# Release of the first expert slots in halves, and a shorter routing chain, in a two-block transformer kernel on one core

## The chip, the cores and the metric

The kernel runs on one core of a Trainium2 chip. The metric is the device time of one execution in microseconds (us). The kernel before takes 778.24 us, the median of 3 runs (778.0 to 778.46).

## The reference

Two transformer blocks of width 1024 over 256 tokens, all in float32. The first block mixes three branches (pooling, latent attention, attention over a memory), adds them to x, and then runs a mixture of experts; the second block is an attention block with a gated feed-forward part. The change lies in the mixture of experts, cut to what matters:

```
g_idx = argmax(g_logits)                       # one of 4 groups, per token
e_sel = e_logits of the 8 experts of that group
top_p, top_i = top_k(softmax(e_sel), 2)
weights = p_g * top_p / sum(top_p)
y = sum over the 2 experts e: weight * (silu(h @ w_gate[e]) * (h @ w_up[e])) @ w_down[e]
```

There are 32 experts, each with a gate matrix and an up matrix of 1024 x 256 and a down matrix of 256 x 1024: three matrices of 1 MiB each. The gains of the norms are folded into the copies that turn the tokens.

## The kernel before, in words

Each engine has its own program, written out by hand in order. They meet at named points: `up(name)` counts a semaphore up, `at(name)` is the wait for it, and `own()` is the wait of an engine for its own last counted instruction.

**Loads.** SyncE (SP) alone issues loads, in one fixed order. Weights go to slots of 1 MiB. A slot is refilled by `fetch` (L496) when the weight in it has been used (`released`). The 96 expert matrices come in the order gate, up, down for each group of four experts; 28 slots are in the ring, so that loads run ahead of the products. The four slots that hold the gate matrices of experts 0 to 3 are refilled in another way, by `fetch_parted` (L504): four quarters each, 2 KB in each of the 128 partitions, quarter by quarter over the four slots, so 16 loads of 256 KB. The quarters wait for the points `taken part 0`, `taken part 1`, `taken part 2` and `taken eg 0`. The matrices that these 16 loads bring are laid out in DRAM in quarters by `laid`. Their place in the queue is behind the load into X (a down matrix, which waits for `h2`) and ahead of the loads into the slots of the up matrices of experts 0 to 3, which wait for `taken eu 0`. The last four up matrices are loaded in halves of 4 KB in each partition by `fetch_last_up` (L514).

**Routing.** VectorE (DVE) works on rows of 4 and 32 numbers for 2 x 128 tokens: logits (L2058), group maximum (L2061), the rank of the first group that has it (L2064, L2067), a mask of the other groups (L2070) which is added to the expert logits (L2074), the two largest of them (L2080), the negated maximum for ScalarE's exponentials (L2083), marking of the two (L2084, L2087), and the 0/1 matrix M (L2090). TensorE (PE) sums M over tokens to give each token its place at its expert (L987 to L989, point `rank`) and the number of tokens of each expert (L991, L992, point `count`). DVE adds the places (L2095) and makes the one-hot matrix `hot` of group 0 (`select`, L2138, point `sel`).

**First expert group.** `begin_experts` on PE waits for `sel 0`, then gathers the tokens of experts 0 to 3 in four parts (`gather_first`, L1021, two of eight tiles of 128 columns each) and multiplies each part by its quarter of the gate matrices (`first_gates`, L1030). DVE copies parts 0 and 1 from PSUM (L2170), ScalarE (ACT) copies parts 2 and 3 (L1610). The order is gather 0, gather 1, gates 0, gather 2, gates 1, gather 3, gates 2, gates 3. Each `first_gates(n)` releases quarter n of the four slots.

**Idle products.** `warm(n, bank)` (L642) issues n matrix products of the constants, whose results nobody reads. `WARM[3]` = 10 of them stand between the logits and the rank, `WARM[4]` = 4 between the count and the first gathering.

**Later groups.** `experts(g)` (L1067) does the gate and up products of group g, `gather(g + 1)` (L1003) gathers for the next one, `experts_down` (L1090) and `combine` (L1100) finish the group. The last group is done expert by expert (L1120, L1129). Behind it the second block follows; its weights are behind the experts' in SP's queue.

Of the kernel before, what the change touches and what calls it, by code (L numbers as in the profile page):

```python
# [10 lines left out]
ALU = mybir.AluOpType  # L11
# [11 lines left out]
FILL_M = 2  # L23
FILL_B = (1, 2, 1, 2) * 3
TILE_AT = {12: 0, 13: 1, 14: 2, 15: 3, 16: 4, 17: 5, 18: 6}
WARM = (9, 6, 9, 10, 4, 6)
FFN_AT = ((0, 0), (1, 0), (2, 0), (3, 0), (6, 0), (7, 0), (0, 1), (1, 1))
CAP = 32
NEG = -1.0e30
# [14 lines left out]
def shape_constants():  # L44
    c = np.zeros((P, C_END), np.float32)
    c[:, C_ID:C_ID + P] = np.eye(P)
    c[:, C_TRI:C_TRI + P] = np.triu(np.ones((P, P)), 1)
    c[:, C_ONE] = 1.0
    causal = np.where(np.tril(np.ones((P, P))) > 0, 0.0, NEG)
    c[:, C_MASK + P:C_MASK + 2 * P] = causal  # L50
    c[:, C_IOTA:C_IOTA + CAP] = np.arange(CAP)
    c[:, C_RANK:C_RANK + 4] = 4 - np.arange(4)
    c[:, C_INVF:C_INVF + 32] = (np.float32(1.0) / (np.float32(10000.0) ** (np.arange(0, 64, 2, dtype=np.float32) / np.float32(64)))).astype(np.float32)
    pool = np.zeros((4, 256, 256), np.float32)
    for g, w in enumerate((2, 4, 8, 16)):
        for s in range(256):
            n = min(s + 1, w)
            pool[g, s + 1 - n:s + 1, s] = np.float32(1.0) / np.float32(n)
            pool[g, s, s] -= 1.0
    pool = np.ascontiguousarray(pool.reshape(4, 2, P, 256).transpose(2, 1, 0, 3)).reshape(P, 2048)  # L60
    return c, pool


class Points:
# [19 lines left out]
    def at(self, name, *key):  # L84
        return (self.sems[name], self.value[name, key]) if self.real else (None, 1)

    def own(self):

        return self.latest
# [22 lines left out]
class Weights:  # L112
# [25 lines left out]
    def plan(self):  # L138


        freed = [u for u in range(self.dense_end) if self.units[u][2]]
        self.slot, self.before, self.nth = [0] * self.dense_end, [None] * self.dense_end, []
        for n, u in enumerate(freed):
            self.slot[u] = n % DENSE
            self.before[u] = freed[n - DENSE] if n >= DENSE else None
        apart = [u for u in range(self.dense_end) if not self.units[u][2]]
        for n, u in enumerate(apart):
            self.slot[u] = DENSE + n
        left = [(self.slot[u], u) for u in freed[-DENSE:]]
        uses = [max(q for q in range(self.dense_pieces) if q % PIECES // 2 == z) for z in range(2)]  # L150
        self.half_first = uses.index(min(uses))
        self.half_use = min(uses)
        near, far = ([(RAW + z, None) for z in (h, 2 + h)] for h in (self.half_first, 1 - self.half_first))
        ring = ([(RAW - 1, None)] + [(self.slot[u], u) for u in apart] + [(RAW + EXT + z, None) for z in (1, 2, 3)]
                + [(RAW + z, None) for z in (8, 9, 4, 5)] + left[:1] + [(RAW + EXT + BIG, None), (RAW + 7, None)]
                + left[1:3] + [(RAW + EXT, None)] + left[3:] + near + far + [(RAW + 6, None), (RAW + EXT + BIG + 1, None)])
        order = [ring[n % len(ring)][0] for n in range(self.expert_end - self.dense_end)]
        held = dict(ring)
        for n, m in ((-16, -4), (-15, -3)):
            order[n], order[m] = order[m], order[n]  # L160
        for u, z in zip(range(self.dense_end, self.expert_end), order):
            self.slot.append(z)
            self.before.append(held[z])
            held[z] = u
        left = [u for u in range(self.expert_end - len(ring), self.expert_end) if self.slot[u] < RAW]
        for u in range(self.expert_end, len(self.units)):
            n = u - self.expert_end
            self.before.append(left[n] if n < RAW else u - RAW)
            self.slot.append(self.slot[self.before[u]])
        times = {}  # L170
        self.parted = [u for u in range(self.dense_end, self.expert_end)
                       if self.key.get(self.before[u]) in [("eg", n) for n in range(4)]]
        self.last_up = [self.raws["eu", n] for n in range(28, 32)]
        for u, z in enumerate(self.slot):
            times[z] = times.get(z, 0) + (64 if u in self.parted else 16)
            self.nth.append(times[z])
        self.final = {}
        for q, p in enumerate(self.pieces):
            self.final[p.unit] = q

    def laid(self):


        self.begin, parts, n = {}, [], 0
        for u, (src, _, _) in enumerate(self.units):
            if not self.dense_end <= u < self.expert_end:
                self.begin[u] = n
                parts.append(np.ascontiguousarray(src).reshape(-1))
                n += parts[-1].size
            elif u in self.parted:  # L190
                self.begin[u] = n
                parts.append(np.ascontiguousarray(src.reshape(P, 4, 512).transpose(1, 0, 2)).reshape(-1))
                n += parts[-1].size
        return np.concatenate(parts)

# [88 lines left out]
def program(nc, ctx, x, xT, mem, memT, positions, gate_b, grow, w_route, b_route, rel_ext, cst, out, wt, dense,  # L284
# [201 lines left out]
    def sync(e, real):  # L486
# [10 lines left out]

        def fetch_parted():

            for a in range(4):  # L500
                for u in wt.parted:
                    e.wait_ge(*(at("taken", "part", a) if a < 3 else released(wt.before[u])))
                    first = wt.begin[u] + 512 * P * a
                    e.dma_start(slot_view(u).rearrange("p k n -> p (k n)")[:, 512 * a:512 * a + 512],  # L504
                                dense[first:first + 512 * P].rearrange("(p m) -> p m", p=P)).then_inc(s_slot[wt.slot[u]], 16)

        def fetch_last_up():

# [120 lines left out]
    def tensor(e, real):  # L629
# [354 lines left out]
        warm(WARM[3], 3)  # L984
        enter(2, "ranked")
        e.wait_ge(*at("M"))
        e.matmul(bank[2][:, 0:32], tri, M[:, 0, :], start=True, stop=True)  # L987
        e.matmul(bank[2][:, 32:64], ones, M[:, 0, :], start=True, stop=False)
        e.matmul(bank[2][:, 32:64], tri, M[:, 1, :], start=False, stop=True).then_inc(*up("rank"))  # L989
        enter(0, "counted")  # L990
        e.matmul(bank[0][:, 64:96], ones, M[:, 0, :], start=True, stop=False)  # L991
        e.matmul(bank[0][:, 64:96], ones, M[:, 1, :], start=False, stop=True).then_inc(*up("count"))  # L992
# [32 lines left out]
        def first_gates(n):  # L1025

            e.wait_ge(*at("XE dve" if n < 2 else "XE act", "part", n))
            for kk in (2 * n, 2 * n + 1):
                for j in range(4):
                    t = e.matmul(bank[0][32 * j:32 * j + 32, 0:256], XE[:, kk, 32 * j:32 * j + 32],  # L1030
                                 slot_view(wt.raws["eg", j])[:, kk, :], start=(kk == 0), stop=(kk == 7))
            t.then_inc(*(up("taken", "part", n) if n < 3 else up("taken", "eg", 0)))

        def begin_experts():

            e.wait_ge(*at("sel", 0))
            e.wait_ge(*at("h2", 1))
            gather_first(0)
            gather_first(1)
            enter(0, "expert a", 0)  # L1040
            for n in range(4):
                e.wait_ge(*landed(wt.raws["eg", n]))
            first_gates(0)
            gather_first(2)
            first_gates(1)
            gather_first(3)
            first_gates(2)
            first_gates(3)
# [711 lines left out]
    def vector(e, real):  # L1760
# [306 lines left out]
        e.tensor_reduce(tm_, OG, AX, ALU.max).then_inc(*routed())  # L2067
        e.wait_ge(*own())
        for i in range(2):
            t = e.tensor_scalar(OG[:, i, :], OG[:, i, :], tm_[:, i, :], NEG, ALU.is_lt, ALU.mult)  # L2070
        t.then_inc(*routed())
        e.wait_ge(*own())
        for i in range(2):
            t = e.tensor_tensor(EM[:, i, :].rearrange("p (g k) -> p g k", g=4),  # L2074
                                el[:, i, :].rearrange("p (g k) -> p g k", g=4),
                                OG[:, i, :].unsqueeze(2).to_broadcast([P, 4, 8]), ALU.add)
        t.then_inc(*routed())
        e.wait_ge(*own())
        for i in range(2):
            t = e.max(top[:, i, :], EM[:, i, :])  # L2080
        t.then_inc(*routed())
        e.wait_ge(*own())
        e.tensor_scalar(nm, top[:, :, 0:1], -1.0, None, ALU.mult).then_inc(*up("expert maximum"))  # L2083
        e.memset(top[:, :, 2:8], ABSENT).then_inc(*routed())  # L2084
        e.wait_ge(*own())
        for i in range(2):
            t = e.match_replace(TT[:, i, :], top[:, i, :], EM[:, i, :], TAKEN)  # L2087
        t.then_inc(*routed())
        e.wait_ge(*own())
        e.tensor_scalar(M, TT, TAKEN, None, ALU.is_equal).then_inc(*up("M"))  # L2090
        e.wait_ge(*own())
        e.tensor_scalar(PX, M, -1000.0, 1000.0, ALU.mult, ALU.add).then_inc(*routed())
# [39 lines left out]
        def select(g):  # L2132

            if g:
                e.wait_ge(*at("gathered", g - 1, 1))
                e.wait_ge(*at("sel weights", g - 1))
            for i in range(2):
                t = e.tensor_tensor(hots[i], iota, of_four(PX[:, i, :], g), ALU.is_equal)  # L2138
            t.then_inc(*up("sel", g))

        def select_weights(g):

# [409 lines left out]
```

## Time and profile before

| | |
|---|---|
| median of 3 runs | 778.24 us (778.0 to 778.46) |
| the profiled execution | 778.07 us, of which the span is 776.3 us |
| PE busy | 731.0 us, 94% of the span |
| DVE busy | 420.0 us, 54% |
| ACT busy | 337.9 us, 44% |
| loads | 206.07 MB, mean 265 GB/s |
| granted TensorE clock, mean | 0.988 |

The span is the time from the first to the last instruction of the trace, and all places in the trace are in us from its start. The granted clock is the part of TensorE's full 2.4 GHz that was granted in a stretch (0.5 is 1.2 GHz). The DMA share is the mean busy share of the 16 DMA engines. The chain that ended last is followed back from the last instruction, at each step to what released it. Rows of TensorE overlap, and in a group the busy time is that of the group, not the sum.

### The profile page before, as it was taken

The page shows a single profiled execution, that of the slowest core. Times are in us where ns is not written, and L with a number is a line of the kernel's source. Part 1 is how long each engine was busy: PE and PEld are TensorE (multiplying, and loading weights), DVE is VectorE, ACT ScalarE, POOL GpSimd, SP SyncE. Part 2 cuts the span into 40 slices and gives each one's busy share as a digit, 9 for nine tenths or more (in the row PEclk, how much of TensorE's full clock was granted, in tenths as well). Part 3 has the DMA queues.
Part 4 walks back from the last instruction along what each step waited for, and adds up shares of the span by engine and source line. Part 5 has one row for each costly group of instructions (what it writes and reads, how often), then busy time and mean ns, then how long its engine had stood idle before and what let it go on. Part 6 is the DMA issues. An engine that isn't in the chain of part 4 may idle for free.

```text
span 776.3 us, 12463 instructions
## 1 busy us (share of the span) xinstructions
PE 731.0 (94%) x5138; PEld 601.7 (78%) x5138; DVE 420.0 (54%) x747; ACT 337.9 (44%) x604; POOL 32.4 (4%) x65
## 2 busy tenths in 40 slices
PE   8999999999999999999675879999999999999997
PEld 8898888888788866666343549999778888888885
DVE  5667756667666421111010208666668776777675
ACT  5966565554444421110010127555656434344433
POOL 2700000000000000000000001000001000000000
PEclk9999999999999999999988999999999999999999
DMA  8953557347988899999999998953434464555201
GB/s 340 415 211 118 206 218 285 120 165 285 372 311 333 342 350 420 421 419 420 421 420 421 413 417 352 422 203 115 157 109 163 159 221 163 193 186 188 84 1 54
DMA packets 34170, 206.07 MB, mean 265 GB/s; under 512 B 4032, under 2 KB 4416, under 8 KB 12352
## 3 DMA queue, kind: packets, MB, share of 16 engines
q1 hardware_dynamic: 34112, 205.25, 68.3%
q8 instruction: 42, 0.69, 0.4%
q14 instruction: 16, 0.13, 0.0%
HBM read 204.18 MB, written 1.05 MB: 264 GB/s over the span
## 4 chain that ended last, share of the span: by engine, by line
PE 79%; DMA 12%; ACT 3%; SPq 3%; DVE 2%; issue 1%; DVEq 0%; POOLq 0%; POOL 0%; ACTq 0%
PE ps L679 43%; PE ps L749 10%; PE ps L752 5%; PE ps L1067 4%; DMA ext<-in_w_up_e 4%; DMA big<-in_w_gate_e 3%; DMA X<-in_w_down_e 3%; PE ps L1090 2%; PE ps L1003 2%; SPq L496 2%; DMA gb<-in_xT 2%; PE ps L1100 1%; PE ps L1192 1%; PE ps L1206 1%; PE ps L1220 1%
## 5 line engine op out<-in xcount | busy, mean ns | idle before, releaser
L1769 DVE TENSOR_TENSOR wl<-raw,wh 128x1024 fp32r<-128x1024 f32 (+3 forms) x181 | 213.3, 1195 | 135.1 <-ACT wh L1352 133.8
L1352 ACT CAST wh<-raw 128x1024 fp32r<-128x1024 f32 (+3 forms) x181 | 181.9, 1024 | 66.4 <-PE ps L679 42.6
L679 PE MATMUL ps<-wh,fra 128*128 128x512 f32 (+3 forms) x636 | 179.2, 367 | 0.5 <-DVE gb L1978 0.5
L679 PEld LDWEIGHTS ps<-wh,fra 128*128 128x128 f32 x636 | 112.8, 189 | 18.2 <-issue 1.0
L679 PE MATMUL ps<-wl,fra 128*128 128x512 f32 (+3 forms) x318 | 115.1, 362 | 0.0
L749 PE MATMUL ps<-fra,wh 128*128 128x512 f32 x352 | 110.7, 396 | 0.7 <-DVE fra L1780 0.7
L752 PEld LDWEIGHTS ps<-fra,wl 128*128 128x128 f32 x352 | 66.1, 188 | 15.5
L679 PE MATMUL ps<-fra,wh 128*128 128x256 f32 x400 | 74.0, 286 | 0.5 <-DVE wl L1769 0.5
L679 PE MATMUL ps<-wh,frb 128*128 128x512 f32 x240 | 74.3, 391 | 0.0
L752 PE MATMUL ps<-fra,wl 128*128 128x256 f32 x352 | 69.2, 278 | 0.0
L679 PEld LDWEIGHTS ps<-wl,fra 128*128 128x128 f32 x318 | 59.9, 188 | 9.0
L679 PEld LDWEIGHTS ps<-fra,wh 128*128 128x128 f32 x400 | 62.3, 191 | 1.9 <-DVE wl L1769 1.2
L2190 DVE TENSOR_TENSOR S<-S,ps 128x256 f32<-128x256 f32 x8 | 3.4, 421 | 98.5 <-ACT S L1619 98.5
L679 PE MATMUL ps<-fra,wl 128*128 128x256 f32 x200 | 56.5, 283 | 0.0
L749 PEld LDWEIGHTS ps<-fra,wh 128*128 128x128 f32 x352 | 54.2, 189 | 1.6 <-issue 0.9
L1067 PE MATMUL ps<-raw,big 128*32 128x256 f32 x400 | 41.6, 390 | 10.9 <-DMA ext<-in_w_up_e 9.1
L679 PEld LDWEIGHTS ps<-wh,frb 128*128 128x128 f32 x240 | 44.1, 188 | 8.5
L1619 ACT ACTIVATE S<-ps 128x256 f32<-128x256 f32 x8 | 3.1, 383 | 106.2 <-PE ps L1067 106.2
L1067 PE MATMUL ps<-big 128*32 128x256 f32 x240 | 41.8, 400 | 6.8 <-DMA ext<-in_w_up_e 6.8
L1067 PE MATMUL ps<-ext,big 128*32 128x256 f32 x320 | 47.1, 407 | 1.1 <-DMA big<-in_w_gate_e 0.8
L679 PE MATMUL ps<-wl,frb 128*128 128x512 f32 x120 | 46.7, 390 | 0.0
L1067 PEld LDWEIGHTS ps<-raw,big 128*32 128x32 f32 x400 | 21.4, 112 | 22.0 <-issue 12.7
(282 smaller groups left out, 992.3 us busy)
## 6 DMA issues: line engine op xcount, KB each, us to landing
raw<-in_dense SPq DMA_DIRECT2D x79, 1024.0 KB, 5.1
ext<-in_w_down_e SPq DMA_DIRECT2D x20, 1024.0 KB, 19.0
raw<-in_w_gate_e SPq DMA_DIRECT2D x17, 1024.0 KB, 25.0
ext<-in_w_up_e SPq DMA_DIRECT2D x14, 1024.0 KB, 24.5
big<-in_w_up_e SPq DMA_DIRECT2D x8, 1024.0 KB, 18.7
big<-in_w_gate_e SPq DMA_DIRECT2D x7, 1024.0 KB, 26.9
raw<-in_w_up_e SPq DMA_DIRECT2D x6, 1024.0 KB, 20.4
raw<-in_dense SPq DMA_DIRECT2D x9, 512.0 KB, 5.3
```

The source lines that it names most:

```text
L496: e.dma_start(slot_view(u).rearrange("p k n -> p (k n)"), src).then_inc(s_slot[wt.slot[u]], 16)
L679: t = e.matmul(o, a, w, start=first and n == 0, stop=final and n == 2, skip_group_check=not check)
L749: e.matmul(bank[b][:, :], h[:, kk, cols[j]], hT_both[:, k], start=(k == 0), stop=(k == 7), skip_group_check=True)
L752: t = e.matmul(bank[b][:, 0:256], l[:, kk, cols[j]], hT[0][:, k], start=False, stop=(k == 7), skip_group_check=True)
L1003: t = e.matmul(bank[2 + a][:, P * (kk % 4):P * (kk % 4) + P], H[:, i, P * kk:P * kk + P], hot[:, P * i:P * i + P], start=(i == 0), stop=(i ...
L1067: t = e.matmul(bank[0][32 * j:32 * j + 32, 256 * half_:256 * half_ + 256], XE[:, kk, 32 * j:32 * j + 32], slot_view(wt.raws[key, 4 * g + j ...
L1090: t = e.matmul(bank[2 + c][32 * j:32 * j + 32, :], AT[z][:, P * k + 32 * j:P * k + 32 * j + 32], slot_view(wt.raws["ed", 4 * g + j])[:, k, ...
L1100: t = e.matmul(turned(k), YE[k // 4][:, P * (k % 4):P * (k % 4) + P], CM, start=False, stop=False, skip_group_check=True)
L1192: t = e.matmul(causal_parts(bank[4 + z])[i], qT[o:o + 64, k, P * i:P * i + P], kT[o:o + 64, k, 0:P * (i + 1)], start=True, stop=True)
L1206: t = e.matmul(bank[7][o:o + 64, cols], H[:, i, 64 * h:64 * h + 64], pt[:, 256 * i:256 * i + 256 - P * i], start=(i == 0), stop=(i == 1))
L1352: e.copy(halves(q)[0], piece_view(q)).then_inc(*up("wh", q))
L1769: e.tensor_tensor(l, piece_view(q), h.bitcast(F), ALU.subtract).then_inc(*up("wl", q))
```

## The change

The four slots of the first gate matrices are given back in two halves instead of four quarters: 8 loads of 512 KB with 4 KB in each partition, the first four waiting for `taken part 1` and the last four for `taken eg 0`. `first_gates(1)` now stands ahead of `gather_first(2)`. The mask of the other groups and its addition to the expert logits become one instruction for each half of the tokens, with a larger constant for the ranks. The negated maximum is computed behind the marking of the two largest instead of ahead of it. The places come from two products (one over 64 columns) instead of three, `select` makes both halves of the one-hot matrix in one instruction (in all eight groups), and `WARM[4]` goes from 4 to 2.

```diff
-WARM = (9, 6, 9, 10, 4, 6)
+WARM = (9, 6, 9, 10, 2, 6)
...
-    c[:, C_RANK:C_RANK + 4] = 4 - np.arange(4)
+    c[:, C_RANK:C_RANK + 4] = -NEG * (4 - np.arange(4))
...
-            times[z] = times.get(z, 0) + (64 if u in self.parted else 16)
+            times[z] = times.get(z, 0) + (32 if u in self.parted else 16)
...
-                parts.append(np.ascontiguousarray(src.reshape(P, 4, 512).transpose(1, 0, 2)).reshape(-1))
+                parts.append(np.ascontiguousarray(src.reshape(P, 2, 1024).transpose(1, 0, 2)).reshape(-1))
...
-            for a in range(4):
+            for a in range(2):
                 for u in wt.parted:
-                    e.wait_ge(*(at("taken", "part", a) if a < 3 else released(wt.before[u])))
-                    first = wt.begin[u] + 512 * P * a
-                    e.dma_start(slot_view(u).rearrange("p k n -> p (k n)")[:, 512 * a:512 * a + 512],
-                                dense[first:first + 512 * P].rearrange("(p m) -> p m", p=P)).then_inc(s_slot[wt.slot[u]], 16)
+                    e.wait_ge(*(released(wt.before[u]) if a else at("taken", "part", 1)))
+                    first = wt.begin[u] + 1024 * P * a
+                    e.dma_start(slot_view(u).rearrange("p k n -> p (k n)")[:, 1024 * a:1024 * a + 1024],
+                                dense[first:first + 1024 * P].rearrange("(p m) -> p m", p=P)).then_inc(s_slot[wt.slot[u]], 16)
...
-        e.matmul(bank[2][:, 0:32], tri, M[:, 0, :], start=True, stop=True)
-        e.matmul(bank[2][:, 32:64], ones, M[:, 0, :], start=True, stop=False)
-        e.matmul(bank[2][:, 32:64], tri, M[:, 1, :], start=False, stop=True).then_inc(*up("rank"))
+        e.matmul(bank[2][:, 0:64], tri, M.rearrange("p i n -> p (i n)"), start=True, stop=False, skip_group_check=True)
+        e.matmul(bank[2][:, 32:64], ones, M[:, 0, :], start=False, stop=True, skip_group_check=True).then_inc(*up("rank"))
...
-            t.then_inc(*(up("taken", "part", n) if n < 3 else up("taken", "eg", 0)))
+            if n % 2:
+                t.then_inc(*(up("taken", "part", n) if n == 1 else up("taken", "eg", 0)))
...
             first_gates(0)
+            first_gates(1)
             gather_first(2)
-            first_gates(1)
             gather_first(3)
...
         for i in range(2):
-            t = e.tensor_scalar(OG[:, i, :], OG[:, i, :], tm_[:, i, :], NEG, ALU.is_lt, ALU.mult)
-        t.then_inc(*routed())
-        e.wait_ge(*own())
-        for i in range(2):
-            t = e.tensor_tensor(EM[:, i, :].rearrange("p (g k) -> p g k", g=4),
-                                el[:, i, :].rearrange("p (g k) -> p g k", g=4),
-                                OG[:, i, :].unsqueeze(2).to_broadcast([P, 4, 8]), ALU.add)
+            t = e.scalar_tensor_tensor(EM[:, i, :].rearrange("p (g k) -> p g k", g=4),
+                                       OG[:, i, :].unsqueeze(2).to_broadcast([P, 4, 8]), tm_[:, i, :],
+                                       el[:, i, :].rearrange("p (g k) -> p g k", g=4), ALU.subtract, ALU.add)
...
-        e.tensor_scalar(nm, top[:, :, 0:1], -1.0, None, ALU.mult).then_inc(*up("expert maximum"))
         e.memset(top[:, :, 2:8], ABSENT).then_inc(*routed())
         e.wait_ge(*own())
         for i in range(2):
             t = e.match_replace(TT[:, i, :], top[:, i, :], EM[:, i, :], TAKEN)
         t.then_inc(*routed())
-        e.wait_ge(*own())
+        taken = own()
+        e.tensor_scalar(nm, top[:, :, 0:1], -1.0, None, ALU.mult).then_inc(*up("expert maximum"))
+        e.wait_ge(*taken)
         e.tensor_scalar(M, TT, TAKEN, None, ALU.is_equal).then_inc(*up("M"))
...
-            for i in range(2):
-                t = e.tensor_tensor(hots[i], iota, of_four(PX[:, i, :], g), ALU.is_equal)
-            t.then_inc(*up("sel", g))
+            e.tensor_tensor(hot.rearrange("p (i e s) -> p i e s", i=2, e=4), iota.unsqueeze(1).to_broadcast([P, 2, 4, CAP]),
+                            PX[:, :, 4 * g:4 * g + 4].unsqueeze(3).to_broadcast([P, 2, 4, CAP]), ALU.is_equal).then_inc(
+                *up("sel", g))
```

## Rows read from the trace of the kernel before

**Rows 1.** The page: span, and GB/s in 40 equal slices.

```profile
span 776.3 us, 12463 instructions
...
GB/s 340 415 211 118 206 218 285 120 165 285 372 311 333 342 350 420 421 419 420 421 420 421 413 417 352 422 203 115 157 109 163 159 221 163 193 186 188 84 1 54
```

**Rows 2.** The chain that ended last, 350 to 490: start us, us, what.

```profile
440.23 21.71 DMA X<-in_w_down_e
461.98 1.07 PE ps L1120 x16
```

**Rows 3.** Busy time in stretches of the expert stage; the last columns are clock, DMA share, GB/s.

```profile
290.00:350.00 60.00, 55.64 (x644) 36.69 (x640) 8.10 (x21) 8.10 (x24) 0.00 (x0) 1.00 1.01 420
350.00:437.00 87.00, 65.10 (x670) 40.91 (x663) 7.95 (x20) 8.70 (x25) 0.00 (x0) 0.90 1.01 421
441.00:445.00 4.00, 2.70 (x44) 1.99 (x48) 0.92 (x4) 0.98 (x2) 0.00 (x0) 1.00 1.03 411
420.00:425.00 5.00, 3.25 (x32) 1.81 (x36) 0.00 (x0) 0.00 (x0) 0.00 (x0) 0.50 1.02 423
268.00:272.00 4.00, 3.06 (x28) 2.90 (x27) 2.82 (x20) 2.69 (x7) 0.00 (x0) 1.00 1.00 422
```

**Rows 4.** The same columns from the tail of the earlier loads to 290.

```profile
275.00:276.00 1.00, 1.00 (x15) 0.63 (x6) 0.54 (x3) 0.00 (x0) 0.00 (x0) 1.00 0.71 287
276.00:279.00 3.00, 3.00 (x37) 2.01 (x40) 0.34 (x2) 0.97 (x4) 0.00 (x0) 1.00 0.69 164
279.00:284.00 5.00, 5.00 (x93) 2.84 (x86) 0.15 (x1) 1.56 (x3) 0.00 (x0) 1.00 1.00 355
284.00:290.00 6.00, 4.54 (x41) 4.11 (x45) 1.60 (x4) 2.11 (x7) 0.00 (x0) 1.00 1.06 406
```

**Rows 5.** SP's queue in order of time: start us, us, the loads issued.

```profile
259.09 0.81 SPq L496 DMA_DIRECT2D ext<-in_w_up_e  x2
...
275.50 1.92 SPq L504 DMA_DIRECT2D raw<-in_dense  x3
...
284.03 1.00 SPq L496 DMA_DIRECT2D big<-in_w_up_e  x2
...
293.26 0.80 SPq L496 DMA_DIRECT2D ext<-in_w_down_e  x2
```

**Rows 6.** The chain that ended last, 267 to 281.

```profile
267.68 0.36 DVE rt L2064 x2
...
268.35 0.37 DVE rt L2070 x2
...
268.74 0.30 DVE rt L2074 x2
...
271.01 0.22 PE ps L989 x2
...
271.68 0.97 PE ps L642 x8
272.65 1.79 PE ps L1021 x16
274.44 1.00 PE ps L1030 x16
...
278.62 1.86 PE ps L1030 x32
```

**Rows 7.** DVE's instructions in order of time around the largest and the first selection.

```profile
269.39 0.17 DVE L2083 TENSOR_SCALAR rt<-rt 128x2 f32<-128x2 f32 x1
269.50 0.07 DVE L2084 MEMSET rt<- 128x12 f32 x1
...
271.60 0.49 DVE L2138 TENSOR_TENSOR big<-C,rt 128x128 f32<-128x128 f32 x2
```

**Rows 8.** Full load rate after an empty queue, columns as in rows 3.

```profile
260.00:264.00 4.00, 4.00 (x26) 3.50 (x25) 2.63 (x4) 1.29 (x4) 0.00 (x0) 1.00 0.95 352
```

## The prediction

> **What bounds the kernel now.** I read the page first: in its slices of 19.4 us the load rate lies at 410 to 422 GB/s from about 291 us to 465 us (but for one at 352), and nowhere else for so long [rows 1]. The chain of waits says the same from the other end. The expert stage does not end with a product: its last group starts at 461.98, just behind a load into X that was issued at 440.23 and took 21.71 us to land [rows 2]. A load that takes so long stood behind others, so the question is whether the queue of loads ever ran dry between the changed place and that end. The table of stretches answers it: 420 and 421 GB/s from 290 to 437, at a DMA share of 1.01, while PE was busy 65.10 of 87 us in the later part [rows 3]. So the end of the expert stage is set by bytes. It moves by as much as the loads are ahead or behind at 290, and by nothing that PE gains meanwhile. The second block behind it runs on PE; its loads stand in the same queue behind the experts' and move with it, so I carry the shift to the end one to one.
>
> The stretches before 290 show where the loads are not full. The rate is 287 GB/s in 275 to 276, 164 in 276 to 279, 355 in 279 to 284, 406 in 284 to 290 [rows 4]. The queue of SP says why: the first quarter is issued at 275.50, at the end of the first gate products (274.44 + 1.00 = 275.44) [rows 5, 6], when the loads before it have almost drained, and the 16 quarters fill the queue until 284.03 [rows 5]. These 15 us carried 287 + 3 x 164 + 5 x 355 + 6 x 406 = 4,990 KB. At 421 GB/s they would have carried 6,315. The shortfall of 1,325 KB is 3.15 us, and that is all that the halves could win.
>
> **Where the loads stand at 290 before.** The 16 quarters are 4,194 KB. I take the 287 KB of the first us as the rest of earlier loads. What is left, 4,990 - 287 - 4,194 = 509 KB, is already of the loads behind them, 1.21 us at 421 GB/s, so the quarters were through at 288.8.
>
> **The release of the first half.** It needs gates 0 and 1, so one block of 1.00 us more than the first quarter needed [rows 6]; against this stands the shorter routing, which starts this block earlier.
>
> - Mask and addition: L2070 starts at 268.35 and L2074 ends at 269.04, 0.69 us for the two pairs [rows 6]. The new pair is of the form of L2064, 0.36 us over 4 columns [rows 6]; with 28 more columns I take 0.42 (between 0.36 and 0.50). Saves 0.27.
> - Negated maximum: without it the memset starts 0.11 us earlier (269.50 - 269.39 [rows 7]). Behind the marking it lies in the wait for that marking, and it may hold M back by as much as it gained. Saves 0.08 (0 to 0.11). ScalarE gets it some 0.2 to 0.5 us later, for exponentials that are used only by the weights, behind the first selection; nothing on the way to the release waits for them.
> - Places: one product pair of three goes, 0.22 us [rows 6]. Saves 0.22 (0.1 to 0.22, as one of the others has 64 columns).
> - Selection: two instructions over 128 columns took 0.49 [rows 7]; one over 256 saves one start. Saves 0.07 (-0.1 to 0.15). In the later groups the selection is off the chain.
> - Idle products: four took 0.97 us and the gathering followed straight behind them, at 272.65 in the chain, 0.56 behind the selection's end (271.60 + 0.49 = 272.09) [rows 6, 7]. With two fewer (0.49), one pair less (0.22) and M 0.35 earlier, PE is free 1.06 us earlier, while the selection is 0.64 earlier in all, so the selection decides now. In place of the 0.56 I put a handover of 0.33 (0.1 to 0.56). Saves 0.23 on top of the 0.64.
>
> Sum 0.87 us (0.4 to 1.2). The first half is released at 275.44 + 1.00 - 0.87 = 275.57 and issued 0.06 later, at 275.63, against 275.50 for the first quarter. Gates 1 needs DVE's copy of part 1; DVE has nothing but the short chain of the weights in between, and part 1 is gathered one block of gates (1.00 us) ahead. Gathering 2 and 3 move behind gates 1, so ScalarE's copies start later, but each lies under the next block of PE's work.
>
> **From the issue to the full rate.** The nearest row is at 259.09, where a load met a drained queue [rows 5]: 260 to 264 carried 4 x 352 = 1,408 KB [rows 8], which is 3.34 us at 421, so the loads ran in effect from 260.66, 1.57 us behind the issue. The halves then start in effect at 277.20. The rate of 4 KB per partition is that of 441 to 445, in the middle of the last up matrices' halves: 411 GB/s [rows 3]. 4,194 KB take 10.20 us and are through at 287.40. **The gain is 288.8 - 287.4 = 1.4 us.**
>
> Does the second half come in time? It waits for gates 3, which end at 278.62 + 1.86 = 280.48 before [rows 6] and some 0.87 earlier now: 279.6. With the same 1.57 us it is there at 281.2, and the first half lasts until 277.20 + 5.10 = 282.3. The margin is 1.1 us. Behind the waiting loads in SP's queue stand the four up loads of 284.03 and the down loads of 293.26 [rows 5], whose own releases come from later products and are thus 0.9 us earlier. The second half keeps the DMA engines busy to 287.4, so these come in time: issued at 283.1 and 292.4, with 4 MiB (10 us) of work behind 287.4.
>
> A rule of the Trainium skill speaks against the term of size: DMA: Bandwidth & Descriptors, Specifications, wants only 512 B or more for the full rate of a transfer, and the quarters have 2 KB. The row disagrees in part: 279 to 284 moved 355 GB/s at a DMA share of 1.00, so the engines were busy without full rate [rows 4]. By that rule the halves would move at 421, 9.96 us, and the gain would be 1.6 us.
>
> The time is made against the profiled execution: 778.07 - 1.4 = 776.7; against the median of 778.24 it is 776.8.
>
> **Rivals.**
>
> *The smaller packets were not the fault.* If the halves move at the mean of the quarters, (5 x 355 + 6 x 406) / 11 = 383 GB/s, they take 10.95 us, end at 288.15, and the gain is 0.65 us: 777.6. For it: in 284 to 290 the quarters reached 406 once enough were queued [rows 4]. Against it: the 411 of the other halves [rows 3].
>
> *The routing shortens by more, or the start is quicker.* A saving of 1.2 us and a first half that fills the queue within 1 us of its issue give a start at 276.3, an end at 286.5 and a gain of 2.3 us: 775.9. For it: each issue now brings twice the bytes. Against it: the 1.57 us at 259.09 were with loads four times a quarter.
>
> *The clock (the other side).* With fewer idle products PE rests more around the routing. In 268 to 272 the clock stayed at 1.00 with PE busy 3.06 of 4 us [rows 3]; elsewhere, in 420 to 425, it was at 0.50 while PE waited for weights [rows 3]. If it fell to 1.2 GHz as the first gathering begins, the 3.79 us of gathering and gates from 272.65 to 276.44 [rows 6] would take 3.79 more, the halves would end at 291.2, and the kernel would lose 2.4 us: 780.6. It decides as soon as the release comes 3.0 us later than I reckon. The new rest of some 0.2 us is small beside the 0.94 us (4 - 3.06) for which PE rests there already. The Trainium skill (TensorE: Matmul & The Clock Gate, Part 1) says that the throttled clock is the default and that activity lifts it, which is the reason to give this rival a chance at all; no row here shows a fall after so short a rest.
>
> *The change does not reach the end.* If the second half came over 1.1 us late, a new hole would open behind the first: with gates 3 at 281.5, 0.8 us of the 1.4 are lost: 777.6, as in the first rival.
>
> **How the numbers follow.** Nothing under 0.2% (1.56 us) can be told from no change here. The forecast (gain 0.9 to 2.0 us, 776.2 to 777.3) has 0.60, the first and the last rival together 0.20, the quick start 0.12, the clock 0.05, and 0.03 stays for a loss that I have not named. The forecast's own range crosses the bound of 776.68, a little less than half of it below. Faster by over 0.2%: 0.28 of the forecast, 0.12 of the quick start, and 0.02 for unnamed gains in the 0.20, so 0.42. Slower: 0.07. The rest, 0.51, is within 0.2%. The range goes from 775.7, a little past the quick start, to 778.2, no gain at all.
>
> **What the next profile would show.** The first half issued at 275.6 (275.3 to 276.1); 8 issues in place of 16, in two lots with a rest near 278 to 279.6; above 400 GB/s from 278 to 290; gates 3 ending near 279.6; the last down load landing 1.4 us earlier (460.5), and the whole second block moved by the same amount. Wrong would be: a first issue after 276.5, a dip below 350 GB/s near 282, a clock below 1.00 in 270 to 285, or a gain at 290 that is gone at 461.

## The result and the profile after

The kernel after takes 782.3 us, the median of 6 runs (781.77 to 783.9), against 778.35 us for the kernel before in the same comparison (777.03 to 779.07, 6 runs). The ratio is 1.0053, with a 95% interval of 1.0043 to 1.0063: slower by 4 us, where I had forecast 1.4 us less and a range that ended at 778.2.

The forecast looked at 275 to 290. The same stretches of the kernel after, as in [rows 4]; the last columns are clock, DMA share and GB/s:

```profile
275.00:276.00 1.00, 1.00 (x11) 0.88 (x8) 0.00 (x0) 0.00 (x0) 0.00 (x0) 1.00 0.38 148
276.00:279.00 3.00, 3.00 (x47) 2.16 (x49) 0.43 (x1) 2.40 (x5) 0.00 (x0) 1.00 0.79 250
279.00:284.00 5.00, 5.00 (x82) 3.41 (x71) 0.92 (x3) 0.85 (x3) 0.00 (x0) 1.00 0.95 356
284.00:290.00 6.00, 4.55 (x44) 3.29 (x47) 0.69 (x1) 1.40 (x5) 0.00 (x0) 1.00 1.03 424
```

In 275 to 290 the loads carried 148 + 3 x 250 + 5 x 356 + 6 x 424 = 5,222 KB, 232 KB more than the 4,990 of [rows 4], which is 0.55 us at 421 GB/s. Another 0.25 us was there before: 240 to 275 moved 356 GB/s against 353, in an execution whose routing began 0.21 us earlier. SP's queue shows the two lots, and the last down load:

```profile
275.25 1.76 SPq L504 DMA_DIRECT2D raw<-in_dense  x3
277.06 0.43 SPq L504 DMA_DIRECT2D big<-in_dense  x1
279.10 1.71 SPq L504 DMA_DIRECT2D raw<-in_dense  x3
...
439.20 2.94 SPq L496 DMA_DIRECT2D X<-in_w_down_e  x1
```

The load into X was issued at 439.20 against 440.23 [rows 2]: 150 us later the loads are still ahead, by 1.03 us. So the loss lies behind that place. The chain of the kernel after, from 441 on (start us, us, what), has no load in it; compare [rows 2], where the load into X was the link to the last group:

```profile
441.39 0.63 PE ps L1111 x4
442.02 5.64 issue
447.66 7.90 PE ps L1067 x96
455.56 1.54 PE ps L642 x12
457.10 1.91 PE ps L1067 x32
...
460.96 1.93 PE ps L1120 x32
```

At 442.02 TensorE stands still for 5.64 us, and "issue" means that it waited for nothing that the profile shows: no semaphore, no load of data. Before, the same place took 0.23 us. The next products are the first of group 7, just behind the branch of L1148 around the general path. TensorE's instructions in order of time, first of the kernel before, then of the kernel after (in brackets the idle time just before the instruction, and what ended it):

```profile
442.07 0.63 PE L1111 MATMUL ps<-C,big 128*128 128x128 f32 x4 [1.30 <-DVE big L2158]
442.93 0.38 PE L1067 MATMUL ps<-ext,big 128*32 128x256 f32 x1 [0.23 <-issue]
```

```profile
441.39 0.63 PE L1111 MATMUL ps<-C,big 128*128 128x128 f32 x4 [1.30 <-DVE big L2155]
447.66 0.60 PE L1067 MATMUL ps<-ext,big 128*32 128x256 f32 x1 [5.64 <-issue]
```

The stretches around it show the second part of the loss (after, columns as above): the clock falls to half during the standstill and stays there while the products of group 7 begin.

```profile
437.00:442.00 5.00, 3.70 (x21) 2.92 (x19) 1.89 (x8) 0.58 (x1) 0.00 (x0) 1.00 1.01 409
442.00:448.00 6.00, 0.36 (x5) 0.23 (x8) 0.00 (x0) 0.58 (x1) 0.00 (x0) 0.55 1.03 410
448.00:453.00 5.00, 5.00 (x53) 2.65 (x48) 0.00 (x0) 0.00 (x0) 0.00 (x0) 0.52 1.02 417
```

One more view tells what TensorE waited for. The table of DMA queues has a line for loads of instructions, 16 KB each (42 of them in either kernel). In 430 to 443, ahead of the branch, the kernel before made one, and the kernel after none. Both made one in 443 to 448; in the kernel after TensorE already stood still then. The queues of before in 430 to 443 (queue: packets, MB, share):

```profile
q1 hardware_dynamic: 955, 5.35, 100.3%
q8 instruction: 1, 0.02, 0.5%
```

Those of after in 430 to 443, where the instruction queue has no line:

```profile
q1 hardware_dynamic: 1021, 5.40, 101.4%
```

And the instruction queue of after in 443 to 448:

```profile
q8 instruction: 1, 0.02, 1.4%
```

Taken in narrower windows, that load stands at 444.82 in the kernel after, 2.80 us behind the start of the standstill, and the products begin 2.84 us behind it. In the three other traces with such a standstill (below) the products begin 2.84 or 2.85 us behind the load.

**The theory** (inferred from these views, then tested; it is called the code placement theory in the expectations). The change takes three products out of TensorE's stream ahead of the branch (one of the places, two idle ones). Every later instruction moves towards the start of the program. The branch jumps over the general path, and what lies behind comes in time only if its load was made before the branch. Before, TensorE had just passed a point in the code at which that load is asked for (I call it the edge below); after, it mostly has not. The Trainium skill (Runtime: NRT & Kernel Launch, Instruction fetch mechanics) states the rule that I had not looked for: instructions are prefetched in sequence in blocks of 16 KiB, and a taken branch whose target is not there has to wait for a load. The traces agree: each load is of 16 KB, and 5.64 us of standstill lie behind the branch where none was made in 430 to 443. The theory's rivals were that the halves or the shorter routing themselves make the wait, and that the two idle products fewer cost the clock.

### The profile page after: what moved, and what is told of

Same layout as the page of the kernel before. It is cut to its first block, busy times and chain, and to the rows that moved or that the text cites. A ratio compares the mean times of both kernels' runs of the same rounds, so it can differ in the third digit from the quotient of the medians.

```text
span 780.2 us, 12433 instructions
## 1 busy us (share of the span) xinstructions
PE 732.2 (94%) x5132; PEld 603.1 (77%) x5132; DVE 419.3 (54%) x737; ACT 338.0 (43%) x604; POOL 32.1 (4%) x65
## 4 chain that ended last, share of the span: by engine, by line
PE 84%; DMA 8%; ACT 3%; issue 2%; DVE 2%; SPq 1%; DVEq 0%; POOLq 0%; POOL 0%; ACTq 0%
PE ps L679 44%; PE ps L749 10%; PE ps L1067 6%; PE ps L752 5%; DMA ext<-in_w_up_e 3%; DMA big<-in_w_gate_e 3%; PE ps L1090 2%; PE ps L1002 2%; PE ps L1100 2%; SPq L496 1%; PE ps L789 1%; PE ps L1192 1%; PE ps L1206 1%; PE ps L1220 1%; DMA raw<-in_dense 1%
## 5 line engine op out<-in xcount | busy, mean ns | idle before, releaser
L752 PEld LDWEIGHTS ps<-fra,wl 128*128 128x128 f32 x352 | 66.2, 188 | 15.5
L1067 PE MATMUL ps<-ext,big 128*32 128x256 f32 x320 | 51.5, 426 | 8.2 <-issue 5.6
L1067 PE MATMUL ps<-big 128*32 128x256 f32 x240 | 46.3, 424 | 8.4 <-DMA ext<-in_w_up_e 8.4
L1067 PE MATMUL ps<-raw,big 128*32 128x256 f32 x400 | 45.6, 415 | 6.2 <-DMA ext<-in_w_up_e 4.5
L679 PEld LDWEIGHTS ps<-fra,wl 128*128 128x128 f32 x200 | 38.4, 192 | 0.0
```

The costliest lines, as they stand in the source:

```text
L679: t = e.matmul(o, a, w, start=first and n == 0, stop=final and n == 2, skip_group_check=not check)
L752: t = e.matmul(bank[b][:, 0:256], l[:, kk, cols[j]], hT[0][:, k], start=False, stop=(k == 7), skip_group_check=True)
L1067: t = e.matmul(bank[0][32 * j:32 * j + 32, 256 * half_:256 * half_ + 256], XE[:, kk, 32 * j:32 * j + 32], slot_view(wt.raws[key, 4 * g + j ...
```

## The experiments

Each was run beside the kernel before, whose medians were 778.05 to 778.38 us. In brackets stands the ratio to it with its 95% interval. Where the executions of a kernel fall in two groups of times, it can lie well below the ratio of the medians (1.0057 against 783.98 / 778.25 = 1.0074 in the second experiment).

**Put back the products, not the work.** Same edits as the kernel after, but three more idle products where TensorE rests:

```diff
-WARM = (9, 6, 9, 10, 2, 6)
+WARM = (9, 6, 9, 13, 2, 6)
```

> The kernel after with 13 idle products instead of 10 between the logits and the rank, so that TensorE's instruction stream has as many products ahead of the branch around the general path (L1148) as the kernel before; the three lie in its rest before M. Code placement theory (the 5.64 us in which TensorE stood still at 442 are a late fetch of the instructions behind that branch, and the slow clock follows from it): the standstill and the half clock at 442 to 453 are gone, the end of the expert stage is where the loads put it, and the kernel takes 777.0 to 777.5 us. Rival, the halves or the routing themselves cause the standstill: it stays, 782 us. Rival, too few idle products lower the clock: those that were taken away behind the count are still missing, so 782 us.

777.48 us (ratio 0.9991, 0.9981 to 1.0001). The load into X is back in the chain, and the clock holds. Its stretches, against those of the kernel after above:

```profile
442.00:448.00 6.00, 5.77 (x100) 3.86 (x100) 0.00 (x0) 0.59 (x1) 0.00 (x0) 1.00 1.03 410
448.00:453.00 5.00, 3.54 (x49) 2.35 (x44) 0.00 (x0) 0.00 (x0) 0.00 (x0) 1.00 1.03 424
```

**Take products out of the kernel before.** The reverse, with none of the change's other edits:

```diff
-WARM = (9, 6, 9, 10, 4, 6)
+WARM = (9, 6, 9, 7, 4, 6)
```

> The kernel before with 7 idle products instead of 10 between the logits and the rank and nothing else: as many products fewer ahead of the branch as in the kernel after. Code placement theory: a standstill of 5 to 6 us behind the branch near 443, half clock behind it, 782 to 784 us. Rivals (halves, routing): 778.3 us as before, since their edits are not in it. Rival clock: TensorE's rest before M grows from 0.9 to 1.3 us and the clock falls near 270, not near 443.

783.98 us (ratio 1.0057, 1.0037 to 1.0076); in its trace 5.8 us of standstill, no load of instructions in 430 to 443, and half clock behind it:

```profile
442.00:448.00 6.00, 0.63 (x4) 0.42 (x4) 0.32 (x2) 0.59 (x1) 0.00 (x0) 0.67 1.03 409
448.00:454.00 6.00, 5.08 (x48) 2.77 (x52) 0.00 (x0) 0.00 (x0) 0.00 (x0) 0.50 1.02 419
```

So the loss comes without halves and without a shorter routing. Two of its 10 executions took 778.83 and 779.41, so by the times the standstill does not come in every execution. The clock was at half in 266.5 to 269.9 too, but this cost nothing at the end of the stage: the load into X was issued at 440.23, as before.

**Take the branch away.** The kernel after with the three lines of the general path removed from TensorE's program; the general path, which these inputs never take, is then missing there.

```diff
-                if real:
-                    with e.If(flag_value > limit):
-                        general_tensor(e)
```

> The kernel after without the branch and the general path on TensorE alone (with these inputs the branch is always taken around it). Code placement theory: no jump, so no standstill at 442 and no slow clock behind it, 777 to 777.5 us. If the standstill were a wait for data or for a semaphore it would stay: 782 us.

777.97 us (0.9993, 0.9983 to 1.0003), and no standstill. No branch, no loss, with as few products as in the kernel after. Its trace has no load of instructions in 430 to 443 either, and one in 443 to 448, yet TensorE did not stand still: a missing load ahead of this place costs nothing without the jump. (Leaving out the general path also moves what lies behind it, so this run alone does not part the jump from the place.)

**Put the products elsewhere.** Three more at the very start of the program:

```diff
-WARM = (9, 6, 9, 10, 2, 6)
+WARM = (12, 6, 9, 10, 2, 6)
```

> The kernel after with 12 idle products instead of 9 at its very start, where TensorE waits for its first weights anyway; everything from the first real product to the end is as in the kernel after. Code placement theory: the same number of instructions ahead of the branch as before, so no standstill near 442, 777 to 778 us. Rival, the three idle products of the first experiment helped by what they do near the routing (clock, rest of TensorE): here they are 265 us away, so the standstill stays, 782 us.

777.22 us (0.9986, 0.9976 to 0.9997). What the idle products do near the routing is thus out. The same kernel again:

> The fifth experiment's kernel again, the best by its median: by code placement no execution near 782, median 777.2 to 777.6 us, a ratio to before of 0.9985 to 0.9995.

777.51 us (0.9996, 0.9984 to 1.0009), 776.12 to 780.21 over 12 executions: no standstill, but the second set is not clear of before.

**How many products.** One more ahead of the rank (`WARM[3]` = 11), twice, and one more at the start (`WARM[0]` = 10):

> The kernel after with 11 idle products instead of 10 between the logits and the rank: one product back of the three. Code placement theory, with a fixed edge somewhere within the three products: either of the two times, 777.5 or 782 to 784 us, and nothing between, but for executions that change over from one to the other. A cause that grows with the number of idle products would give two thirds of the loss, some 781 us in every execution.

> The sixth experiment's kernel again, as the base of the two others on the same chip: 777.2 us by code placement, and no execution near 782.

> The kernel after with 10 idle products instead of 9 at the very start and nothing else, the smallest mend. Code placement theory, with the result of one more idle product ahead of the rank: 777.2 us, faster than before by 0.8 to 1.2 us.

777.22 (0.9987, 0.9976 to 0.9998), 777.66 (0.999, 0.9977 to 1.0004) and 777.51 us (0.9991, 0.9979 to 1.0003). One product is enough: the edge lies between three and two products fewer than before. Now to the other side, `WARM[0]` = 6, three fewer than after:

> The kernel after with 6 idle products instead of 9 at the very start: six products fewer ahead of the branch than before, three fewer than after. Code placement theory: still on the wrong side of the edge, 782 us. A cause that counts idle products: worse than the kernel after.

782.65 us (1.0026, 1.0005 to 1.0048); 5.8 us of standstill in the trace, and 5 of its 8 executions over 781. And half a block the other way, 32 idle products in a wait of group 6:

```diff
                 parted = half_ and g == 7
+                if half_ and g == 6:
+                    warm(32, 3)
```

> The kernel after with 32 idle products while TensorE waits for the up matrices of group 6 (410 to 421 in the trace of before). They move the branch by half a block of 16 KB of code, and keep TensorE busy where the clock fell to 0.50 at 419. Code placement theory: past the edge, so no standstill, 777 to 778 us; the clock at 419 does not matter, as the loads set the pace there. If only the exact place of before is good, the standstill comes back: 782 us or more.

My expectation failed: 779.71 us (1.0015, 1.0003 to 1.0026). The profiled execution has 2.67 us of "issue", not right behind the branch but among the first products of group 7, and the clock stays up:

```profile
440.93 0.38 PE L1069 MATMUL ps<-ext,big 128*32 128x256 f32 x1 [0.20 <-DMA big<-in_w_gate_e]
...
446.35 0.41 PE L1069 MATMUL ps<-raw,big 128*32 128x256 f32 x2 [2.67 <-issue]
```

No load of instructions was made in 430 to 443 here either, and one at 443.78. From the last product ahead of the branch (it ends at 440.73) to the restart at 446.35 it is 5.62 us, as in the kernel after (5.64). In between TensorE had some 2.8 us of products behind the branch that it could run; so the code just behind the branch was there and only what follows it was missing (inferred). So there is more than one edge, and I have not mapped them. This execution took 776.89 us and is the fastest of the eight; what the others did, with 778.4 to 781.29, no trace shows.

**How often.** The kernel after once more:

> The kernel after again, to see in how many executions the standstill comes. In the kernels with three products fewer ahead of the branch than before it was there in 8 of 10, 5 of 8 and 7 of 10 executions by their times, and in 6 of 6 of the kernel after. If the edge is a matter of chance in each execution, some of the executions here take 777 to 779 us; if the kernel after lies wholly on the wrong side, all take 781 us or more.

782.45 us (1.005, 1.0029 to 1.007). Ten of 12 executions took 782.05 to 786.63, two took 777.91 and 778.19. Together: of 36 executions of kernels with three or six products fewer than before, 29 took over 781 us. Of the 84 of the kernels with products put back (one or three; quarters and quarter-quarter-half below among them) and the 10 of the kernel before with halves, none did. The kernel before itself did in 4 of the 150 executions beside the experiments (781.15 to 782.48), of which no trace was kept.

The traces say the same. Of the 20, four have the standstill of 5.6 to 5.8 us right behind the branch, and none of these has a load of instructions in 430 to 443. All 14 traces of kernels with the branch that have one there are without it (three of them have a delay of mine in its place), and so is the kernel without the branch; the last trace is the one with 32 products in group 6.

**What the loss consists of.** The kernel with one more idle product has no standstill. In it I held TensorE behind the branch by a wait of my own:

```diff
+                e.wait_ge(*at("held"))
...
+        e.wait_ge(*at("CM turned", 7, 1))
+        for n in range(8):
+            e.memset(S[2], 0.0).then_inc(*(up("held") if n == 7 else up("pool step", "hold", n)))
+            e.wait_ge(*own())
```

The lines at the end are GpSimd's, which clears an unused tile eight times, one after the other.

> The kernel with one more idle product ahead of the rank (no standstill, 777.2 us), in which TensorE is now held behind the branch on purpose: it waits for 8 fills of an unused tile by GpSimd, some 5.3 us, which begin when the last weights are turned. If the loss of the kernel after is nothing but TensorE standing still there, this kernel shows the same: half clock from 443 to 453 and 781.5 to 783 us. If a late start at this place were covered by the wait for the last loads, it would take 777 to 779 us.

781.95 us (1.0037, 1.0018 to 1.0056; 7 executions): a wait of 4.7 us makes nearly the loss of the kernel after again. The end of the wait, from its chain:

```profile
446.44 0.53 POOL S L2449
446.97 0.04 issue
447.01 8.10 PE ps L1067 x96
455.11 1.53 PE ps L642 x12
```

Next, idle products in place of the wait, `warm(48, 3)` and then `warm(24, 3)`:

> The same kernel with 48 idle products (5.5 us at full clock) at the same place instead of the wait. TensorE is as late as in the held kernel, but never at rest. By the rows of after, the half clock cost 7.90 - 5.28 = 2.6 us in the 96 products behind the standstill. If that is right, the clock stays at 1.00 and the kernel takes 2.6 us less than the held one, 779 to 780 us. If the slow clock is not what costs, both take the same.

> The fourteenth experiment mended: an idle product there took 10.89 / 48 = 0.227 us, not 0.115, so 24 of them are the 5.5 us that were meant. Split of the loss as reckoned from the fourteenth (96 products took 5.32 us at full clock against 8.10 in the held kernel): the clock stays at 1.00, the 96 products start near 446.5, and the kernel takes 2.0 to 2.8 us less than the held one, 779.2 to 780 us. If the slow clock were not part of the loss: 782 us.

The first gave 783.81 us (1.0074, 1.0048 to 1.01; 4 executions), and no split, since I had taken one product for 0.115 us where it is 0.227: 10.89 us of lateness. Its clock stayed at 1.00, and the 96 products took 5.32 us. The second, 5.54 us of idle products, gave 779.86 us (1.0026, 1.0017 to 1.0036), 2.1 us less than the held kernel. Chain of the second:

```profile
441.67 5.54 PE ps L642 x48
447.20 5.32 PE ps L1067 x96
452.52 1.53 PE ps L642 x12
```

Both begin group 7 at the same time (447.01 and 447.20), one at a clock of 0.54 in 447 to 453 and one at 1.00. So of the 4.3 us between the held kernel and its base (781.95 - 777.66, the one product more), 2.1 is the clock and 2.2 is lateness. The two ran on different chips; against the kernels before beside them the clock's part is 1.8 us, and the intervals of the two ratios overlap, so the split is rough. The 8.10 and 5.32 us of the 96 products are what shows that the clock has a part.

It also gives what TensorE had to spare. The second kernel came 5.54 - 0.23 = 5.3 us late and lost 2.2: 3.1 spare. The held one came 4.7 + (8.10 - 5.32) = 7.5 late and lost 4.3: 3.2 spare. The kernel after, 5.64 - 0.23 + (7.90 - 5.32) = 8.0 late, should then lose 4.9 against the mended kernels' 777.5, and lost 4.8; so close an agreement is in part luck. (The first, 10.7 late, lost only 6.1; I can't say why it comes off better.)

The spare time could have been read from the trace of before, without a run. In 441 to 463 TensorE's waits for loads are 2.6 us together; in the six traces of the mended kernels they are 1.7 to 2.7, and the trace of after has none. The waits of before (who waited for whom: us in total, times, longest):

```profile
PE ps L1067 <- DMA ext<-in_w_up_e: 2.0, 2, 1.8
...
PE ps L1120 <- DMA ext<-in_w_down_e: 0.3, 1, 0.3
PE ps L1120 <- DMA X<-in_w_down_e: 0.3, 1, 0.3
```

**Let TensorE arrive early.** To see the standstill without the wait on loads around it, no idle products in the last places of the up loads:

```diff
-WARM = (9, 6, 9, 10, 2, 6)
+WARM = (9, 6, 9, 10, 2, 0)
```

> The kernel after without the 6 idle products between the halves of the last up matrices (L1062), which stand behind the branch, so the code ahead of it does not move. In the kernel before they fill a wait for loads; in the kernel after, by the theory, TensorE is so late behind its standstill that it waits for no load any more and their 1.54 us lie on the chain. Theory: the standstill stays, 782.3 - 1.5 = 780.8 us. If loads or a semaphore still set the end in the kernel after, it stays at 782.3 us.

780.35 us (1.0026, 1.0012 to 1.004), and inconclusive: its profiled execution was one without a standstill, so the chain that I wanted to see is not in it. Of its 10 executions three took 778.35 to 778.8 and seven 780.08 to 782.37; the median of the seven, 781.41, is 1.2 us below that of the 16 executions over 781 of the kernel after (782.59), where I expected 1.5. The trace is of use all the same. Ahead of the branch the code is that of the kernel after, and here the load of instructions came in 430 to 443 and TensorE did not stand still: the same code ahead of the branch goes either way.

**The parts of the change, with the code where it was.** Halves and the new order of gates in the kernel before; quarters and the old order in the first experiment's kernel; and quarter, quarter, half in it:

```diff
+            for a, (c0, c1) in enumerate(((0, 512), (512, 1024), (1024, 2048))):
                 for u in wt.parted:
+                    e.wait_ge(*(at("taken", "part", a) if a < 2 else released(wt.before[u])))
```

> The kernel before with the halves and the new order of gates and gatherings alone; routing, places and idle products as before, so the number of products ahead of the branch is unchanged. Code placement theory: no standstill. The first half is released one block of gates later than the first quarter, at 276.4, and by the sum of the prediction the parted loads are through at 288.3 instead of 288.8: 777.5 to 778.5 us. If halves as such make the kernel slow: 782 us.

> The first experiment's kernel with the four quarters and the order of gates and gatherings of before: the shorter routing alone, with the code where it was. The first quarter is released 0.9 us earlier (near 274.5), before the loads ahead of it have drained, so the hole of 276 to 279 shrinks; the rest moves with 2 KB per partition. By the rows of before the quarters are through near 288.1: 777.5 us, within 0.5 us of the first experiment. If the halves matter by themselves, the first experiment is better by over 0.7 us.

> The first experiment's kernel with the four slots given back in a quarter, a quarter and a half (12 loads), the order of gates and gatherings as in the kernel after. The first quarter is issued at the end of gates 0, near 274.4, when loads are still in flight, so the hole of the load queue at 276 closes, and the last half keeps its 4 KB per partition. Expected 1.0 us less than the first experiment: 776.5 us. If the start of a load after an empty queue costs nothing, no difference: 777.5 us.

778.1 (0.9994, 0.9985 to 1.0004), 777.87 (0.9996, 0.9984 to 1.0007) and 778.0 us (1.0001, 0.9989 to 1.0012). Neither part can be told from no change by itself, nor can the third kernel, which missed my 776.5. It was to close the hole at 276 by an earlier quarter, but in its trace the hole was not closed: the first quarter was issued at 275.28, no earlier than the first half after (275.25), 275 to 276 moved 8 GB/s, and the clock was at half for part of the routing (0.73 in 266 to 268, 0.61 in 268 to 271). What a closed hole is worth was not seen.

## Why the prediction was wrong

**The step that failed** is "by nothing that PE gains meanwhile", and with it "so I carry the shift to the end one to one". The bound by loads holds only as long as TensorE comes in time for the last ones. It had 2 to 3 us to spare there (2.6 by the waits in the trace of before, 3.1 and 3.2 by the kernels with a delay put in), and came 8 late. That PE was busy 65.10 of 87 us ahead of this place [rows 3] says nothing of it: in that time TensorE had waited for loads already, and none of it is left for the last group. I priced the removed products by the time that they took and by what they delay, and at nothing for what they do to the code behind them: it cost 5.64 us of standstill and 2.6 us of half clock. None of my rivals had this in it. The clock rival named a cause of the right sign at a wrong place (270 instead of 443) and for a wrong reason: the clock fell because TensorE stood still, not because idle products were missing.

**The routing** was right, a little small: the release came at 275.25 where [rows 6] give 276.44 + 0.06 without a gain. Of these 1.25 us 0.21 are an earlier start of the whole routing (the first logits at 266.98 against 267.19), so 1.04 against the 0.87 of the sum. The new pair took 0.42 us, the single selection 0.42. Most of the difference is the handover: the gathering began 0.19 us behind the selection's end (271.41 - 271.22), where I had put 0.33. By the chain it again follows straight behind the idle products, so it is not the selection that decides, as I had it, but the two are within 0.2 us of each other.

**The load term** was mis-sized. I took 411 GB/s for the halves from a row with a full queue. In 279 to 284 they moved 356, no more than the quarters' 355, where I had expected over 400; in the 16 traces with two halves this stretch has 314 to 406, 361 in the mean. (The lower rate in 281 to 282, 332, was one of my signs of being wrong.) In 284 to 290 it was 424. The gain in 275 to 290 was 0.55 us in this profile, not 1.4; in six traces of the mended kernels (one or three more products), by the same sum and against the one trace of before, it is 0.4 to 1.5. Their medians measure it better, without the standstill: 0.5 to 0.8 us less than before in all six comparisons, 0.1%, in four of them not clear of none. The rival "the smaller packets were not the fault" had priced it at 0.65 us. What the size of the loads does by itself is not shown, since no run changes it alone.

**The second half in time**: right, issued at 279.10 (predicted 279.6). **The order of gates, the waits, the negated maximum**: no wait of theirs shows on the way to the release, as reckoned.

## What to carry to other kernels

Here three products fewer ahead of a branch cost 4.8 us, and the change that took them out is worth 0.5 to 0.8. In another program with a branch on an engine, look for "issue" time right behind a branch, compare the loads of instructions around it, and test it by adding idle instructions far away, where nothing else changes: if the time jumps, what was measured is the place of the code and not the edit. When a stage is bound by loads, say also how late the other engine may be before it takes over; its own waits for loads in the last group give the number.

## What the runs showed of the hardware

- TensorE stood still for 5.6 to 5.8 us behind its branch, in 4 traces (the kernel after twice, and the two kernels with three idle products fewer), when the load of 16 KB of instructions came only afterwards; the products began 2.84 or 2.85 us behind that load. In one placement TensorE stood still for 2.7 us, among the products behind the branch, again until 5.62 us behind the last product ahead of it. The loads of weights filled the DMA engines all the while (share 1.03, 408 to 410 GB/s). That this makes the load of instructions slow was not tried.
- The same program gave both times from execution to execution (777.91 and 778.19, against ten from 782.05).
- Standing still for 4.7 to 5.8 us took the clock to 1.2 GHz (0.50 to 0.54 behind it); 5.54 us of idle products in its place kept it at 2.4 GHz (1.00).
- Near the routing the clock fell in some executions and not in others of the same kernel: with three more products at the start it was 1.00 in 266 to 271 in one trace, and 0.50 and 0.77 in 266 to 268 and 268 to 271 in the other. It was 1.00 throughout in the kernel after, but not in the kernel without the branch, whose code is the same up to there (its stretches, columns as above). There the first half was issued at 276.60, not at 275.25:

```profile
266.00:268.00 2.00, 2.00 (x18) 2.00 (x17) 0.67 (x3) 2.00 (x2) 0.00 (x0) 0.85 1.01 422
268.00:271.00 3.00, 3.00 (x16) 3.00 (x16) 2.21 (x16) 3.00 (x8) 0.00 (x0) 0.53 1.01 423
```
